# Two norms taken out of stages of their own, a choice among 64 sums in place of 256, and row work spread evenly

## The reference, cut to what matters

```python
h = rmsnorm(x, norm_mix_g); proj = einsum('bsd,de->bse', h, w_in)       # first layer, first step
...
x = x + merged @ w_out[l]                                               # second layer
h2 = rms_norm(x, g_ffn[l])
q = (hf @ w_q).reshape(T, 8, 2, 128)                                    # 8 heads, two halves
sc = einsum('thpd,hpkd->thpk', q, subkeys)                              # 128 keys a half
s1, i1 = top_k(sc[:, :, 0], 16);  s2, i2 = top_k(sc[:, :, 1], 16)       # both in falling order
cand = s1[..., :, None] + s2[..., None, :]                              # 16 x 16 sums a head
top_s, pos = top_k(cand, 16);  idx = (i1 * 128 + i2) at pos
gate = softmax(top_s)
act = gelu(einsum('chkd,cd->chk', u[idx], h))                           # 128 of 16384 experts a token
out = einsum('chk,chkd->cd', gate * act, v[idx])
```

## Time and profile before

| | us |
|---|---|
| median of 3 runs | 2891.82 |
| the runs | 2889.8 to 2896.16 |
| the profiled execution | 2895.71 |
| its span, first to last instruction | 2893.8 |
| TensorE busy in the span | 2790.9 |
| VectorE busy | 2038.1 |

### The profile page before, as it was taken

How to read it: one execution, slowest core, us unless ns; L and a number is a source line. 1 busy time by engine, 2 the same in 40 slices (tenths; PEclk the granted TensorE clock), 3 DMA queues, 4 the chain that set the end, 5 groups by cost and what they waited for, 6 DMA issues and landing times. The chain is left out here.

```text
span 2893.8 us, 36724 instructions
## 1 busy us (share of the span) xinstructions
PE 2790.9 (96%) x13965; PEld 2367.8 (82%) x13965; DVE 2038.1 (70%) x3268; ACT 1380.3 (48%) x2185; POOL 413.1 (14%) x293
## 2 busy tenths in 40 slices
PE   7999999899999999989999999999999899999999
PEld 5756888578888688968788789999999888888887
DVE  4476533388888625776653688898887868888886
ACT  4336522277777615765432433367666543233332
POOL 0000000000100100000000000211112335544552
PEclk9999999799999999999999999999999999999999
DMA  4100262557677621121242324677778979999996
GB/s 168 52 23 1 83 172 90 233 204 298 260 294 273 235 109 52 60 97 45 92 138 81 141 104 135 226 253 266 271 271 327 358 279 391 392 391 392 393 389 261
DMA packets 165854, 600.48 MB, mean 208 GB/s; under 512 B 15792, under 2 KB 87088, under 8 KB 137392
## 3 DMA queue, kind: packets, MB, share of 16 engines
q1 hardware_dynamic: 106928, 436.08, 41.3%
q0 software_dynamic: 41472, 138.45, 12.9%
q10 hardware_dynamic: 17280, 23.60, 2.2%
HBM read 563.96 MB, written 71.86 MB: 220 GB/s over the span
## 5 line engine op out<-in xcount | busy, mean ns | idle before, releaser
L2730 POOL DMA_INDIRECT RG<-in_un,EI x128 | 182.6, 1427 | 1242.9 <-DVE EI L2982 842.4
L2730 POOL DMA_INDIRECT RG<-in_vn,EI x128 | 184.1, 1439 | 257.6 <-DVE X L2744 230.7
L3101 PE MATMUL bank<-VH,GL 128*128 128x512 f32 x768 | 208.5, 393 | 0.4 <-DVE GL L2796 0.4
L3097 PE MATMUL bank<-VH,GH 128*128 128x512 f32 x768 | 208.0, 392 | 0.0
L2744 DVE SCALAR_TENSOR_TENSOR X<-RG,DG,X 128x1024 f32<-128x1024 f32 x128 | 164.2, 1283 | 42.6 <-DMA RG<-in_vn,EI 38.7
L2741 DVE CUSTOM_DVE_ANT_0 RG<-RG,HR 128x1024 f32<-128x1024 f32 x128 | 156.5, 1223 | 36.1 <-DMA RG<-in_un,EI 35.4
L2711 PE MATMUL bank<-HTl,UH0r 128*128 128x384 f32 x512 | 175.8, 343 | 0.2 <-ACT UH0r L2696 0.2
L2711 PE MATMUL bank<-HTl,UH1r 128*128 128x384 f32 x512 | 175.9, 344 | 0.0
L2712 PE MATMUL bank<-HTh,UH1r 128*128 128x384 f32 x512 | 172.0, 336 | 0.0
L2712 PE MATMUL bank<-HTh,UH0r 128*128 128x384 f32 x512 | 171.4, 335 | 0.0
L3101 PEld LDWEIGHTS bank<-VH,GL 128*128 128x128 f32 x768 | 144.1, 188 | 33.2 <-DVE GL L2796 0.9
(11 more groups left out here) (718 smaller groups left out, 7695.6 us busy)
## 6 DMA issues: line engine op xcount, KB each, us to landing
UR<-in_u SPq DMA_DIRECT2D x64, 1024.0 KB, 7.1
VR<-in_vn SPq DMA_DIRECT2D x32, 2048.0 KB, 10.0
UP<-in_wup SPq DMA_DIRECT2D x22, 2048.0 KB, 8.1
DN<-in_wdn SPq DMA_DIRECT2D x32, 1024.0 KB, 7.0
wspill<-VR SPq DMA_DIRECT2D x12, 2048.0 KB, 8.3
aspill<-GA ACTq DMA_DIRECT2D x120, 192.0 KB, 5.3
W<-in_weights SPq DMA_DIRECT2D x10, 2048.0 KB, 11.2
HT<-in_wup SPq DMA_DIRECT2D x10, 2048.0 KB, 7.5
```

Source lines behind the costliest of these rows:

```text
L2730: e.indirect_dma_start(RG[q % RR], None, d["un" if what == "u" else "vn"][:, :], off).then_inc(*row_in[q % RR].up(16))
L3097: e.matmul(bk, r(gh[:, a, t]), r(vh[:, a, :]), start=g == 0 and a == 0, stop=False)
L3101: e.matmul(bk, r(gl[:, a, t]), r(vh[:, a, :]), start=False, stop=False)
```

## The change

1. **Start.** The block of the first norm is gone; its work stands in the block of the input products. x is loaded in four DMAs, the 128 columns of the identity and the 8 gains of this norm ahead of the rest, weight tile 0 in four quarters. The norm is done in two groups of two token blocks; group 0 is turned and split first, weight tile 0 is split between the groups, the first product (token block 0) stands before group 1's turn. The table of ScalarE's functions is loaded at the start, while x is on its way.
2. **The product keys' norm.** For token blocks 0 to 2, squares, root and scaling stand in `Late`, each behind the addition that completes its block of x. Block 3's norm stands in the next block behind the first product of u. The 11 filler matmuls are gone. The first tile of u is loaded and split in `Late`.
3. **The choice.** Since both lists of 16 fall, the 16 best of the 256 sums lie among 64 of them: row 0 with 16 columns, rows 1 to 3 with 8, rows 4 to 7 with 4, rows 8 to 15 with 1. `dve_chosen` forms and searches these 64. Part 6, which turned a position into row and column with 4 instructions, takes 14.
4. **One-hot rows.** The two instructions of `dve_hot` (512 elements a partition each) become one of 1024.
5. **Pace.** `FIRSTS` has a second product in step 0; `TURNS` goes from 0.66 and 1.25 rows a step to 0.8 and 1.0. Rows done in the steps: 95 before, 96 now. The turn of chosen experts (`pe_chosen`, part 13) of token blocks 1 and 2 stands three steps later.

```diff
-            with ExitStack() as c1:
-                norm = Norm(c1, "mix", 0, 0, None, "mix")
...
+                def act_squares(e, g):
+                    for b in (2 * g, 2 * g + 1):
+                        e.wait_ge(*x_in[b](16))
+                        e.activation((kbT, qbT)[g].rearrange("p a n -> p (a n)")[:, span(b % 2, 1024)], xm[b], ACT.Square, accum_out=m_ss[:, b:b + 1]).then_inc(*m_sq.up(1))
+                    e.wait_ge(*m_var(g + 1))
+                    e.activation(m_o[:, span(g, 2)], m_v[:, span(g, 2)], ACT.Sqrt).then_inc(*m_root.up(1))
...
                     def _(e):
+                        e.wait_ge(*in_id(16))
+                        pe_turns(e, 0)
                         for step in range(45):
...
+                                if n == 1:
+                                    pe_turns(e, 1)
+                                    e.wait_ge(*in_c(16))
+                                if n == 2:
+                                    e.wait_ge(*m_lo(12))
...
                     def _(e):
-                        for j in range(4):
-                            dve_quarter(e, 0, j)
+                        dve_roots(e, 0)
+                        dve_rows(e, 0)
+                        dve_roots(e, 1)
+                        e.wait_ge(*in_g0(16))
+                        dve_columns(e, 0)
+                        dve_quarter(e, 0, 0)
+                        dve_quarter(e, 0, 1)
+                        dve_rows(e, 1)
+                        dve_quarter(e, 0, 2)
+                        dve_quarter(e, 0, 3)
+                        dve_columns(e, 1)
...
                         o = X[:, u % 4, span(u // 4, 512)]
                         e.tensor_tensor(o, o, bank[OUT_BANK[u]], ALU.add).then_inc(*self.x_add.up(1))
+                        if 4 <= u < 7:
+                            e.wait_ge(*self.x_add(u + 1))
+                            dve_norm_rows(e, u - 4)
+                        if u == 5:
+                            e.wait_ge(*f_hi(1))
+                            e.tensor_tensor(r(UR0[1]), UR0[0], UH0, ALU.subtract).then_inc(*f_lo.up(1))
...
+                PAIRS = ((0, 1, 16, 0), (1, 4, 8, 16), (4, 8, 4, 40), (8, 16, 1, 56))
...
-                    for a, dst in enumerate((OA[n % 3], OB[n % 3])):
-                        i = e.tensor_tensor(dst, cc("iota").unsqueeze(1).to_broadcast([128, 4, 128]), IA[:, a, span(n, 4)].unsqueeze(2).to_broadcast([128, 4, 128]), ALU.is_equal)
-                    i.then_inc(*h_one.up(1))
+                    to = [128, 2, 4, 128]
+                    e.tensor_tensor(OAB[n % 3], cc("iota").unsqueeze(1).unsqueeze(1).to_broadcast(to), IA[:, 0:2, span(n, 4)].unsqueeze(3).to_broadcast(to),
+                                    ALU.is_equal).then_inc(*h_one.up(1))
...
-                FIRSTS = [1.0] * 8 + [3.0] + [1.0] * 14 + [1.2] * 14
+                FIRSTS = [2.0] + [1.0] * 7 + [3.0] + [1.0] * 14 + [1.2] * 14
                 FIRSTS += [0.88] * 64
                 FIRSTS += [(128 - LAST - sum(FIRSTS)) / 34] * 34 + [1.0] * LAST
-                TURNS = [0.0] * (NQ + 14) + [0.5] * 14 + [0.66] * 66 + [1.25] * 32 + [0.5] * LAST
+                TURNS = [0.0] * (NQ + 14) + [0.5] * 14 + [0.8] * 66 + [1.0] * 32 + [0.5] * LAST
...
-                        warm(e, 6, 7)
-                        norm.pe_turn(e)
-                        e.wait_ge(*n_keptV(4 + 4))
-                        warm(e, 5, 0)
-                        e.wait_ge(*n_keptV(4 + 8))
+                        for k in range(8):
+                            if k >= 6:
+                                e.wait_ge(*s_lo(k - 5))
+                            for tb in range(3):
+                                i = e.transpose(bank[TURN_BANK[k]][:, span(tb)], XR[tb][:, span(k)], ident)
+                            i.then_inc(*s_turn.up(1))
                         for step in range(NQ + NM):
                             for q in firsts(step):
                                 pe_first(e, q, bank[place(q)], last_at(q))
+                                if q == 0:
+                                    e.wait_ge(*s_rows(4))
+                                    for p in range(2):
+                                        for j in range(4):
+                                            i = e.transpose(bank[4 + p][:, span(j)], XR[3][:, span(4 * p + j)], ident)
+                                        i.then_inc(*s_turn.up(1))
```

More of the change, by code:

```diff
@@ L666, in _ @@
                     def _(e):
+                        rows = d["x"].rearrange("(b p) n -> p b n", p=128)
+                        put = lambda c: (C[:, c], d["consts"][:, c])
+                        id0, id1 = CONST["ident"][0], CONST["ident"][0] + CONST["ident"][1]
+                        assert id0 == 0
+                        for b in range(4):
+                            e.dma_start(xm[b], rows[:, b, :]).then_inc(*x_in[b].up(16))
+                            if b == 1:
+                                e.dma_start(*put(slice(0, id1))).then_inc(*in_id.up(16))
+                        g0 = slice(GAIN["mix"][0], GAIN["mix"][0] + GAIN["mix"][1])
+                        e.dma_start(G[:, g0], d["gains"][:, g0]).then_inc(*in_g0.up(16))
+                        for j in range(4):
+                            c = slice(2 * j * 488, (2 * j + 2) * 488)
+                            e.dma_start(W2[0][0][:, c], w_src(0)[:, c]).then_inc(*(w0_in[j] if j < 3 else w_in[0]).up(16))
+                        loaded[0] = 1
+                        e.dma_start(*put(slice(id1, NCONST))).then_inc(*in_c.up(16))
+                        assert g0.start == 0
+                        e.dma_start(G[:, g0.stop:NGAIN], d["gains"][:, g0.stop:NGAIN]).then_inc(*in_g.up(16))
                         load_weights(e, 10)
@@ L1184, in program @@
             with ExitStack() as c1:
-                norm = Norm(c1, "ffn", 1, 1, HT, "ffn", rows=XN)
+                norm = Norm(c1, "ffn", 0, 0, HT, "ffn", rows=XN)
                 ME, msq = sb("ME", [128, 2, 1024], c1), sb("msq", [128, 1024], c1)
@@ L2821, in program @@
                 QS = [RG[3][:, span(n, 256)] for n in range(3)]
-                norm = Norm(cx, "ffn2", 2, 3, None, "ffn2", rows=RowsOf(RG))
+                gain = gg("ffn2")
+                s_turn, s_hi, s_lo = sems("s_turn s_hi s_lo")
+                TURN_BANK = (2, 3, 4, 5, 6, 7, 2, 3)
                 p_wh, p_wl, p_q, p_qt, p_sc, p_sk, p_top = sems("p_wh p_wl p_q p_qt p_sc p_sk p_top")
@@ L3046, in program @@
                         MATCH[28 + 32 * (tb - 1) + 2 * part].append((tb, part))
+                FLIPS = [[] for _ in range(NM)]
+                for step, done in enumerate(MATCH):
+                    for tb, part in done:
+                        if part == 13 and tb < 3:
+                            FLIPS[step + (3 if tb else 0)].append((tb, part))
                 hot = lambda step: step - 28 if 28 <= step < 28 + 96 else None
                 outer = lambda step: step - 30 if 30 <= step < 30 + 96 else None
-                FIRSTS = [1.0] * 8 + [3.0] + [1.0] * 14 + [1.2] * 14
+                FIRSTS = [2.0] + [1.0] * 7 + [3.0] + [1.0] * 14 + [1.2] * 14
                 FIRSTS += [0.88] * 64
                 FIRSTS += [(128 - LAST - sum(FIRSTS)) / 34] * 34 + [1.0] * LAST
-                TURNS = [0.0] * (NQ + 14) + [0.5] * 14 + [0.66] * 66 + [1.25] * 32 + [0.5] * LAST
+                TURNS = [0.0] * (NQ + 14) + [0.5] * 14 + [0.8] * 66 + [1.0] * 32 + [0.5] * LAST
                 ROWS1 = round(sum(TURNS))
@@ L3187, in _ @@
                             if step >= NQ:
-                                for tb, part in MATCH[step - NQ]:
+                                for tb, part in FLIPS[step - NQ]:
                                     pe_chosen(e, tb, part)
@@ L3214, in _ @@
                                     act_outer(e, o)
-                                for tb, part in MATCH[step - NQ]:
+                                for tb, part in [m for m in MATCH[step - NQ] if m[1] == 12] + FLIPS[step - NQ]:
                                     act_chosen(e, tb, part)
```

216 lines of the change are left out of this document (146 added, 70 removed).

## The result

| | before | after |
|---|---|---|
| median, beside each other | 2893.99 us (4 runs) | 2860.21 us (4 runs, 2852.52 to 2865.68) |
| ratio | | 0.9878, 95% interval 0.9861 to 0.9896 |
| the profiled execution | 2895.71 | 2852.52 |
| the same kernel once more, with the experiments | 2898.71 (13 runs) | 2859.21 (4 runs), ratio 0.9867, 0.9848 to 0.9886 |

The change makes the kernel 34 us faster, with 2857.4 forecast and 2846 to 2872 as its range. The profiled execution of after is the fastest of its four, so the two profiles differ by 43.1 us, 9 more than the medians.

The account below looks back on a forecast made before the run. TensorE, busy 2790.9 of 2893.8 us, was taken as the bound, with some 103 us idle. Gains of 9.3 + 13.1 + 1 + 11 = 34.4 us, off the median 2891.82, gave 2857.4 us, range 2846 to 2872.

Parts of the forecast that it names:

- Start: First norm and input products: first product 12.6 us sooner, less 3.3 for group 1's turns; gain 9.3 us, ends 5 and 12.6.
- Product keys' norm: Norm moved into `Late`, one more product of u done before the queries: gain 13.1 us, ends 8 and 14.
- 0.8 us ahead of need: At the queries: the split of query weights and small columns end near 1611.6, 0.8 us before TensorE needs them.
- The choice and its spot: Searching 64 sums saves VectorE 29 us; only TensorE's 1.4 us idle at 1760 to 1800 counts: gain 1, ends 0 and 2.
- Pace: Late stretch, 2220.5 to 2360.6 us: fewer gathered rows move 11.3 us of DMA time out; gain 11, ends 6 and 18.
- The 66 steps and the one-hot rows: Steps ahead of the late stretch: more rows cost 0, ends 0 and 4; merged one-hot rows save VectorE 0 to 0.16 us a step.
- The late loss stays: Late stretch: bursts, not the sum of bytes, stop VectorE before a row; gain 23.4, 2868.4 us, chance 0.14.
- The late loss goes whole: Late stretch: rows are late only above half of 365 GB/s, so none is; gain 41.4, 2850.4 us, chance 0.15.
- The clock: Without fillers, product 0 and products of u run partly at 1.2 GHz, costing 4.2 + 4; gain 26, 2865.6 us, chance 0.12.
- Slower: Denser rows upset the 66 steps, 8 spills at 4.5 us each: 13 us slower, 2904.4 us, chance 0.03.

## Why the prediction was right

The forecast was a gain of 34.4 us, and the medians gave 33.8 and, in the second comparison, 39.5. The mechanisms of the start and of the norm were right, that of the pace in part, and one step failed. That the sum came out this close is partly luck: start, norm and pace gave 2.4, 1.2 and 4.2 us more than forecast, and the third term 8.5 less.

1. *Start*, 9.3 forecast, 11.7 in the profile, 12.6 alone by the medians. The first product came at 16.19, 16.4 forecast, and the second at 25.08, 27.7 forecast. What was off is the turns of group 1: 3.3 us forecast at 0.207 each, 1.91 measured, and they overlap the next product, which starts 1.67 behind their first. The rate of the earlier trace rows doesn't hold here: 16 turns in 1.91 and 24 in 2.92 us are 0.12 each. Why the turns at the start of the kernel before took 0.207 isn't shown, as the trace has no record of the clock ahead of 24.1 us; those of the norm took 0.174 by the clock (next term).
2. *Product keys' norm*, 13.1 forecast, 14.3 measured. The queries were to start 14.2 us behind the block's start and start 12.8 behind it. What was off is the rate of the turns again: 24 were to take 4.2 us and take 2.9. The prediction took 0.174 each from the earlier trace rows without looking at the clock there, which was 0.51 for 16 of its 29. The cover "0.8 us ahead of need" held, as nothing waits there, and without the additional product it is 3.4 us short.
3. *The choice and its spot*, +1 forecast, -7.5 measured. This step failed. VectorE saves the 29 us that were forecast (28 measured), and the wait at that spot is 1.4 us before and with the norm alone and 0.3 with one product fewer, where the sums ahead of the split take 0.90 us in place of 2.29; that fits the forecast 1, though no run has the choice alone. But with the additional product the pauses are as long with the choice among 256 as among 64. The working looked at what VectorE saves, and not at what the additional product moves: "one product more in step 0" was counted in the norm's term as cover alone. It also shifts the split of the tiles of u by a step against the parts of the choice behind it. Taking the product back later (2.0 for 3.0) takes the pauses away, and so does not giving it (the old first numbers); taking back the pace, the one-hot rows or the choice leaves them.
4. *Pace*, 11 forecast, 15.2 in the profile, 16 to 18 by medians. The working took the moved DMA time for the gain and kept 7 us as bursts. But the DMAs are no less busy after: their share is 0.90 in the 161 us of either kernel, at 336 and 340 GB/s. The loss has one path: VectorE waits for a row, and the one-hot rows stand behind it. With fewer rows asked for in a step, nearly all of it goes (1.8 us left, 7 forecast).
5. *The 66 steps and the one-hot rows*, 0 forecast, and no idle time there; two one-hot instructions cost nothing that can be told.

The rivals. *The late loss stays* is out (1.8 us left). *The late loss goes whole* had the better number for its term (18 against 11, 15.2 measured), but not the mechanism: a threshold at half the bandwidth would leave no row late at 170 GB/s, below its 183, and there VectorE's lateness still costs 5.0 us of waits. The Trainium skill (DMA: Bandwidth & Descriptors, Queues, rings and completion order) says that an engine goes round the queues that have work. No run here tests that; the half for each of two queues, which the prediction read out of it, didn't tell when a row is late. *The clock* at the norm is out: 1.00 from 1578 to 1593 us with no filler, where the kernel before lost 1.7 us of it in the turns. At product 0 it is 0.76 (16.2 to 23.4 us), and 0.67 before (29 to 37). The clock was lost elsewhere, behind the two pauses. *Slower* is out: the 66 steps took 0.8 and even 0.9 of a row.

Open: what lengthens the unchanged stages beside the clock, by up to 4 us; whether the turns at the start of the kernel before were slow by the clock; and the 6 us by which the two comparisons of after and before differ in their medians, within their intervals.

## What to carry to other kernels

Where two kinds of work with different periods stand in the in-order list of one engine (here a split every second product and a part of the choice every step), one more piece at the front changes which stands ahead of which everywhere behind it: print the order at each later place where an engine waits, and give the piece back as soon as its cover is no longer needed. What an engine saves is worth nothing until an instruction that is waited for moves up. And where an engine in order waits for transfers, the wait can grow faster than the rate that is asked for (1.2, 5.0 and 15.6 us at 1.0, 1.14 and 1.25 rows a step): spread the asking until the wait is gone, and no further. Before a duration is carried from one stage to another, look at the granted clock beside it.

## What the runs showed of the hardware

- A wait of TensorE of 3.2 to 3.4 us in full work brought each time a stretch of lower granted clock that began about its end (at 1740 to 1760, at 1870 to 1890, and at the queries without the additional product). It lost 1.7 us mostly (a mean of 0.83 over 10 us) and 3.4 us twice (choice among 256, norm alone), so such a wait costs 5 to 7 us. Waits of 0.3 to 1.4 us in the first two places cost no clock.
- The clock lost in unchanged stages differs between two executions of one kernel by 6.7 us (18.8 and 25.5 us), nearly the 6.8 by which their spans differ. Over all thirteen profiles it is 18.8 to 27.3 us.
- Turns (transposes of 128x128, f32) took 0.21 us each at a granted clock of 0.51 and 0.10 to 0.12 at 1.00.
- Eight MAX8 of 64 columns start and end in 1.11 us, 0.14 each; the mean duration of one, 0.21, counts their overlap. Elementwise instructions of 128 elements took 0.22 to 0.32, where 0.2 was forecast.
